# Products for the 64 sampled tokens with 64 stationary columns instead of 128, and their attention probabilities turned from 64 rows, in a hybrid encoder step

## What is computed

```
# attention: prompt frames see chunks of 64, sampled frames see 512 cached rows and themselves
p = jax.nn.softmax(sc, axis=-1)
outs.append(jnp.einsum('bhqk,bkhd->bqhd', p, v[:, :kend]))
# retention, per chunk
att = jnp.einsum('bihd,bjhd->bhij', qc, kc) * dmat
y = (jnp.einsum('bhij,bjhe->bihe', att, vc)
     + jnp.einsum('bihd,bhde->bihe', qc, S) * cross[None, :, :, None])
# mLSTM, per chunk
sc = jnp.einsum('bthd,bshd->bhts', qc, kc) * jnp.exp(dm - m_t[..., None])
num = jnp.einsum('bhts,bshe->bhte', sc, vc) + g[..., None] * jnp.einsum('bthd,bhed->bhte', qc, C)
```

## Time and profile before

| | us |
|---|---|
| median of 3 runs | 933.67 |
| lowest and highest | 933.37 and 934.33 |
| the profiled execution | 933.06 |
| its span, first to last instruction | 931.3 |
| TensorE busy, share of the span | 922.5 (99%) |
| TensorE's weight loads busy | 811.5 (87%) |
| DVE, ACT and POOL busy | 495.3, 204.2 and 444.4 |

### The profile page before, as it was taken

How to read it: one execution, slowest core, us unless ns; L and a number is a source line. 1 busy time by engine, 2 the same in 40 slices (tenths; PEclk the granted TensorE clock), 3 DMA queues, 4 the chain that set the end, 5 groups by cost and what they waited for, 6 DMA issues and landing times.

```text
span 931.3 us, 14894 instructions
## 1 busy us (share of the span) xinstructions
PE 922.5 (99%) x5718; PEld 811.5 (87%) x5718; DVE 495.3 (53%) x1009; ACT 204.2 (22%) x445; POOL 444.4 (48%) x469
## 2 busy tenths in 40 slices
PE   8999999999999999999999999999999999999998
PEld 6777877777999999999977678777799999999998
DVE  5474656854565656512253565578357565563221
ACT  2224264531100000100031243562310000110001
POOL 6210380124966666676411205503168666666670
PEclk9999999999999999999999999999999999999999
DMA  9959412119544544443443773112555555534321
GB/s 279 231 132 69 141 47 91 50 15 253 137 136 137 137 137 139 133 146 125 123 128 108 61 147 95 46 48 50 124 149 140 142 144 144 148 123 135 126 95 41
DMA packets 159635, 113.02 MB, mean 121 GB/s; under 512 B 10246, under 2 KB 157356, under 8 KB 159436
## 3 DMA queue, kind: packets, MB, share of 16 engines
q1 hardware_dynamic: 154660, 104.50, 38.8%
q0 software_dynamic: 4272, 6.80, 7.1%
q10 hardware_dynamic: 632, 0.75, 0.3%
HBM read 108.46 MB, written 2.27 MB: 119 GB/s over the span
## 4 chain that ended last, share of the span: by engine, by line
PE 97%; DVE 1%; DMA 1%; ACT 0%; issue 0%; SPq 0%; ACTq 0%; DVEq 0%
PE ps L1128 52%; PE ps L776 20%; PE ps L1085 7%; PE ps L1146 2%; PE ps L885 1%; PE ps L857 1%; PE ps L982 1%; PE ps L922 1%; PE ps L1023 1%; PE ps L1032 1%; PE ps L804 1%; PE ps L824 1%; PE ps L965 1%; DMA arena<-in_x_sample 1%; PE ps L1043 1%; PE ps L1064 0%
## 5 line engine op out<-in xcount | busy, mean ns | idle before, releaser
L776 PE MATMUL ps<-hT,ring 128*128 128x320 f32 x672 | 187.8, 435 | 2.2 <-DVE hT L1597 1.7
L776 PEld LDWEIGHTS ps<-hT,ring 128*128 128x128 f32 x672 | 124.5, 190 | 54.8 <-DVE hT L1597 3.9
L601 POOL TENSOR_TENSOR work<-ring 128x512 f32<-128x512 f32 (+1 forms) x66 | 81.8, 1239 | 154.5 <-issue 113.3
L1128 PE MATMUL ps<-mixT,ring 128*128 128x160 f32 x672 | 105.0, 299 | 0.0
L1128 PE MATMUL ps<-hT,work 128*128 128x160 f32 x672 | 98.5, 299 | 0.0
L1128 PE MATMUL ps<-hT,ring 128*128 128x160 f32 x672 | 98.1, 299 | 0.0
L1128 PEld LDWEIGHTS ps<-mixT,ring 128*128 128x128 f32 x672 | 95.8, 190 | 0.0
L1128 PEld LDWEIGHTS ps<-hT,ring 128*128 128x128 f32 x672 | 93.7, 190 | 0.3
L1128 PEld LDWEIGHTS ps<-hT,work 128*128 128x128 f32 x672 | 93.7, 190 | 0.0
L603 POOL TENSOR_TENSOR work<-ring 128x512 f32<-128x512 f32 (+1 forms) x66 | 82.2, 1246 | 5.2
L602 POOL TENSOR_TENSOR ring<-ring 128x512 f32<-128x512 f32 (+1 forms) x66 | 82.2, 1246 | 5.2
(11 more groups left out here) (392 smaller groups left out, 1351.6 us busy)
## 6 DMA issues: line engine op xcount, KB each, us to landing
ring<-in_w_gu SPq DMA_DIRECT2D x88, 512.0 KB, 5.2
ring<-in_w_in SPq DMA_DIRECT2D x44, 512.0 KB, 7.1
ring<-in_w_down SPq DMA_DIRECT2D x32, 512.0 KB, 4.5
ring<-in_w_out SPq DMA_DIRECT2D x16, 512.0 KB, 4.5
ring<-in_w_down SPq DMA_DIRECT2D x16, 384.0 KB, 3.5
cst<-in_consts POOLq DMA_DIRECT2D x1, 1664.0 KB, 12.3
ring<-in_w_in SPq DMA_DIRECT2D x2, 640.0 KB, 5.5
arena<-r POOLq DMA_DIRECT2D x8, 160.0 KB, 17.0
```

Of the source, the lines that this page charges most:

```text
L601: step(tt(s3, a11, a21, ALU.subtract))
L776: ins = mm(bank(use, 0, T, m), w[:, k, c:c + m], hT[:, k, 0:T], start=(k == 0), stop=(k == KT - 1))
L1128: ins = mm(bank(use, at * HT, HT), left, right(k), start=(opens and k == 0 and at == 0), stop=(closes and k == n - 1), skip_group_check=True)
```

## The change

The sampled tokens' part of the scores, outputs and turned probabilities is cut to the 64 columns or rows that hold something. L806 takes 64 stationary columns of the keys and writes 64 partitions. The two products of `head_out` for the sampled tokens take 64 stationary columns and write 64 partitions (their lines become L818 and L819, and L824 becomes L825). In `turn_probs` the transpose of the tokens' own keys goes from 64 rows and 64 columns, and the four of the cached keys from 64 rows and 128 columns, with 64 columns of the identity moving; their results lie side by side, 64 columns each. ACT's copies and the slices in `weigh_values` follow, and DVE multiplies 64 partitions of the sampled tokens' scores.

```diff
@@ -62,7 +62,7 @@
 NQ = KT // 2
 MIXES = FT - 1 + 3 * NQ
 MSLOTS = 3
-SCORE_PARTS = ((0, 384), (448, 64))
+SCORE_PARTS = ((0, 384, P), (448, 64, DEC))
 WARM = 12
 
 
@@ -803,7 +803,7 @@
                 q, k = qh[:, h, :], kf[:, h // 2, :]
                 mm(bank(use, 0, 256), k[:, 0:128], q[:, 0:256], start=True, stop=True)
                 mm(bank(use, 256, 128), k[:, 128:256], q[:, 128:256], start=True, stop=True)
-                fill(mm(bank(use, 448, 64), k[:, 256:384], q[:, 256:320], start=True, stop=True), use)
+                fill(mm(bank(use, 448, DEC, DEC), k[:, 256:256 + DEC], q[:, 256:320], start=True, stop=True), use)
 
             def head_out(use, l, h, wready, e, state, cross, mlstm):
 
@@ -814,8 +814,9 @@
                 mm(o(0), w[:, 0:128], vaug[:, 0, h, 0:e], start=True, stop=True)
                 mm(o(1), w[:, 128:256], vaug[:, 0, h, 0:e], start=True, stop=False)
                 mm(o(1), w[:, 256:384], vaug[:, 1, h, 0:e], start=False, stop=True)
-                mm(o(2), w[:, 448:576], vaug[:, 2, h, 0:e], start=True, stop=False)
-                mm(o(2), cross, state, start=False, stop=True)
+                last = bank(use, 2 * e, e, DEC)
+                mm(last, w[:, 448:512], vaug[:, 2, h, 0:e], start=True, stop=False)
+                mm(last, cross, state, start=False, stop=True)
                 for s, tiles in enumerate(((0, 1), (2,))):
                     for t in tiles:
                         a, b_ = vw[:, h % 2, t, 0:e], ktm[:, t, h * HD:(h + 1) * HD]
@@ -997,7 +998,7 @@
                         need(pe, "ktm_d", l, 1)
                         need(pe, "vaug_d", l, 2)
                         need(pe, "qg_d", l, 1)
-                    head_out(f"do{h}", l, h, "w_d", HD + 1, ct[:, l, h, :], qg[:, h, :], True)
+                    head_out(f"do{h}", l, h, "w_d", HD + 1, ct[:, l, h, :], qg[:, h, 0:DEC], True)
 
                 def between(h):
                     if h == 0:
@@ -1026,10 +1027,12 @@
                     u = f"bp{h}"
                     claim(pe, u, l)
                     need(pe, "probs", l, H, h + 1)
-                    for a, w_, rr in ((0, 128, 128), (128, 128, 128), (256, 128, 128), (448, 64, 64),
-                                      (512, 128, 128), (640, 128, 128), (768, 128, 128), (896, 128, 128)):
-                        dst = bank(u, 384 if a == 448 else a, 128, rr)
-                        ins = nc.tensor.transpose(dst, pr[:, a:a + w_], ident)
+                    for a in range(0, 3 * P, P):
+                        nc.tensor.transpose(bank(u, a, P), pr[:, a:a + P], ident)
+                    nc.tensor.transpose(bank(u, 3 * P, DEC, DEC), pr[0:DEC, 448:512], ident[0:DEC, 0:DEC])
+                    for i in range(4):
+                        ins = nc.tensor.transpose(bank(u, 512 + i * DEC, DEC), pr[0:DEC, 512 + i * P:512 + (i + 1) * P],
+                                                  ident[0:DEC, 0:DEC])
                     fill(ins, u)
 
                 def weigh_values(h):
@@ -1040,7 +1043,7 @@
                     mm(bank(u, 64, 64), pT[:, 128:256], vb[:, 0, h, :], start=True, stop=False)
                     mm(bank(u, 64, 64), pT[:, 256:384], vb[:, 1, h, :], start=False, stop=True)
                     for i in range(4):
-                        mm(bank(u, 128, 64, DEC), pT[:, 512 + i * P:512 + i * P + DEC], vb[:, 3 + i, h, :],
+                        mm(bank(u, 128, 64, DEC), pT[:, 512 + i * DEC:512 + (i + 1) * DEC], vb[:, 3 + i, h, :],
                            start=(i == 0), stop=False)
                     fill(mm(bank(u, 128, 64, DEC), pT[0:64, 384:384 + DEC], vb[0:64, 2, h, :], start=False, stop=True), u)
 
@@ -1094,7 +1097,7 @@
                         feature(f"lg{h}", l, "lg", h * P, P)
                     else:
                         project(h - 2, (6, 7, 2, 3))
-                    head_out(f"co{h}", l, h, "w_c", HD, s0c[:, l, h // 2, :], qg[:, h, :], False)
+                    head_out(f"co{h}", l, h, "w_c", HD, s0c[:, l, h // 2, :], qg[:, h, 0:DEC], False)
                     if h == 0:
                         turn_out("bT", l, ybm, "y_b")
                 for n in range(2, 4):
@@ -1459,8 +1462,8 @@
                         wait_filled(act, f"bo{h - 1}", l)
                     u = f"bp{h}"
                     step(A(pT[:, 0:384], bank(u, 0, 384), ACT.Copy))
-                    step(A(pT[0:64, 384:512], bank(u, 384, 128, 64), ACT.Copy))
-                    step(A(pT[:, 512:1024], bank(u, 512, 512), ACT.Copy), "pT")
+                    step(A(pT[0:DEC, 384:384 + DEC], bank(u, 384, DEC, DEC), ACT.Copy))
+                    step(A(pT[:, 512:512 + 4 * DEC], bank(u, 512, 4 * DEC), ACT.Copy), "pT")
                     now_read(act, u)
 
                 def conv_input(k):
@@ -1868,8 +1871,9 @@
                 for h in range(H):
                     need(dve, "decay_d", l, H, h + 1)
                     wait_filled(dve, f"ds{h}", l)
-                    for a, n in SCORE_PARTS:
-                        step(v.tensor_tensor(wt[:, h % 2, a:a + n], bank(f"ds{h}", a, n), dh[:, h % 2, a:a + n], ALU.mult))
+                    for a, n, r in SCORE_PARTS:
+                        step(v.tensor_tensor(wt[0:r, h % 2, a:a + n], bank(f"ds{h}", a, n, r), dh[0:r, h % 2, a:a + n],
+                                             ALU.mult))
                     now_read(dve, f"ds{h}")
                     step(tails(h, dh[:, h % 2, :], HD + 1), "w_d")
                     if h + 1 < H:
@@ -1983,8 +1987,8 @@
                 def weights_c(h):
                     step(tails(h, dec[:, h, :], HD))
                     wait_filled(dve, f"cs{h}", l)
-                    for a, n in SCORE_PARTS:
-                        step(v.tensor_tensor(wt[:, h % 2, a:a + n], bank(f"cs{h}", a, n), dec[:, h, a:a + n], ALU.mult),
+                    for a, n, r in SCORE_PARTS:
+                        step(v.tensor_tensor(wt[0:r, h % 2, a:a + n], bank(f"cs{h}", a, n, r), dec[0:r, h, a:a + n], ALU.mult),
                              "w_c" if a else None)
                     now_read(dve, f"cs{h}")
```

## The result

| | before | after |
|---|---|---|
| median of 14 runs, us | 933.46 | 935.61 |
| lowest and highest, us | 933.04 and 935.17 | 935.32 and 937.39 |
| ratio, 95% interval | | 1.0026, 1.0019 to 1.0033 |
| span of the profiled execution, us | 931.3 | 933.8 |

A forecast was written before the change was run, and what follows sets the result against it. TensorE's own order was taken as the path, each switch costing 0.093 us and a bare load. Scores +3.3, mLSTM +0.6, retention -1.7, turn +0.6, waits -0.1 made +2.7 us: 936.4 us, range 935.0 to 938.0.

The forecast's parts named there:

- What bounds the kernel: Whole kernel: TensorE, busy 99% of the span at full clock, is the path; gains of ACT, DVE and POOL are worth nothing.
- Scores, +3.3: L806, 16 times: new switches and bare loads cost 0.235 us at each of 14 places, +3.3 us.
- the two places ahead of ACT's wait: Head 0 of retention, once a layer: the loss fits into TensorE's 0.28 us idle before L804, costing nothing.
- mLSTM, +0.6: mLSTM outputs, 8 times: switches on both sides of the narrowed products, +0.076 us each, +0.6 us.
- retention, -1.7: Retention outputs, 8 times: both switches are paid already, so narrowing gains 0.211 us each, -1.7 us.
- the sign given, 0.33 from L818 to L825: mLSTM profile after: L818 and L819 should take about 0.33 us from start to the start of L825.
- The turn, +0.6 less 0.1 for the waits: Turned probabilities, 8 times: +0.08 us each on TensorE, +0.6; four waits of 0.04 us before L1039 disappear, -0.1.
- The sum: Whole kernel: all terms together +2.7 us, giving 936.4 us; chance 69%.
- Rival 1: New switch places: no switch price is paid, only savings stand, -5.9 us, 927.8 us; chance 4%.
- Rival 2: Turned probabilities: 64-row transposes switch free, the turn gives -1.7 for +0.6, total +0.4, 934.1 us; chance 13%.
- Rival 3: Turned probabilities: one more switch between the 64*64 and 64*128 transposes, total +3.9, 937.5 us; chance 14%.

The follow-up runs named there:

- the turn's own run: Only the turn of the probabilities from 64 rows, with ACT's smaller copies and packed slices, against the kernel before: 933.44 us, ratio 1.0002.

## Why the prediction was right

- *What bounds the kernel.* Right. ACT lost 2.7 us of work and DVE none (495.7 us busy for 495.3), with no effect but at the waits before L1039; the clock stayed full, and what follows the touched stages took as long as before.
- *Scores, +3.3.* +3.2 in the stretch; 0.23 instead of 0.235 a place (the four terms written there add up to 0.233). That the two places ahead of ACT's wait cost nothing was right in kind; the idle time shown fell to 0.19 and not to 0.1, because the switch back (0.093) now lies in what the record calls idle: 0.28 - 0.185 + 0.093 = 0.19.
- *mLSTM, +0.6, and retention, -1.7.* +0.6 and -1.7. In mLSTM the sign given, 0.33 from L818 to L825, did not fit the forecast's own terms, which make 0.38 (0.109 + 2 x 0.059 + 0.152); 0.37 was measured.
- *The turn, +0.6 less 0.1 for the waits.* +0.15 together, for +0.5. On TensorE each turn cost 0.07, for 0.08 as priced. The term that was mis-sized is the waits: I counted the 0.04 of idle time and left out that a load behind a wait lies bare. Without the wait it is hidden again, 0.07 more at each of the four places, so 0.4 us came back and not 0.1. It is the same effect that I had priced behind every switch.
- *The sum.* 2.7 forecast, 2.2 in the stretch and between the medians. The forecast time was 0.8 too high: 0.35 by the turn's waits, 0.2 because it stood on a median of three runs, 933.67, that came to 933.46 over fourteen, the rest by the small terms.
- *Rival 1 (no price at the new places)* is refuted by retention's gain beside mLSTM's loss, and by 64 against 65 columns. *Rival 2 (64-row transposes switch free)* is refuted by the 0.20 us from the last pass of L1031 to L1032 (122.61 and two times 0.109, to 123.03) and by the turn's own run, which would have given -1.7. That the total came out below the forecast is the waits, and nothing of this rival. *Rival 3 (a switch from 64*64 to 64*128 in transposes)* is refuted by the 0.08 us from L1032 to L1034. The Trainium skill (TensorEngine Tiling, Restrictions and Gotchas) excludes column tiling from f32 transposes, and this agrees; its Key Properties speak of a drain at a change of mode, and if these switches are such changes, the 0.093 us at each new one are its price here.

## What to carry to other kernels

Half a tile is cheap only among neighbours of its own kind. Where TensorE is the path, read the distances between starts at each change of the stationary shape: a change between more than 64 and at most 64 rows or columns cost 0.093 us (in transposes, the rows alone) and a load that nothing hides, more than the columns it saved in runs of two to five passes. A narrow product next to one that is narrow already, as in retention, gained. Either put the narrow products side by side, or keep them at 65 columns, or at full rows with zeros; and count what a wait costs with the load behind it.

## What the runs showed that I had not expected

- One padding column (65 for 64) turned a loss of 3.5 us into a gain of 0.9 for the scores. Used throughout, with the rows of one product filled up to 128, it gave 925.61 us against 933.35, 0.8% less, with more columns loaded than needed.
- A wait of 0.04 us cost 0.11, since the load behind it lay bare (L1039 before, L1042 after).
- Gains of TensorE of some 7 us pass through to the end; at 8.3 us the DVE chain behind the recurrence began to bind (0.41 us idle a layer), and behind it the feed-forward products met waits for DVE and POOL.
